# Feed-forward stages on split fp32 weights: low parts read from PSUM, high parts on GpSimd, block sums on VectorE, a fourth old-form pair

## What is computed

```python
def swiglu(x, w_in, w_out):
    a, b = jnp.split(x @ w_in, 2, axis=-1)
    return (jax.nn.silu(a) * b) @ w_out
...
x = x + 0.5 * swiglu(rmsnorm(x, norm_ffn1[i]), ffn1_w_in[i], ffn1_w_out[i])
```

## Time and profile before

| | |
|---|---|
| median of 3 runs | 3021.34 us (3018.04 to 3023.96) |
| the profiled execution | 3024.76 us, span 3023.1 us |
| TensorE busy | 2721.4 us, 90% of the span |
| VectorE busy | 2184.2 us, 72% |
| ScalarE busy | 1185.7 us, 39% |
| Pool busy | 1352.3 us, 45% |
| mean granted TensorE clock | 0.959 |

### The profile page before, as it was taken

One profiled execution on the slowest core, in us unless ns is written; L12 is line 12 of the kernel. 1 busy time (PEld: TensorE's weight loads), 2 busy tenths in 40 slices (PEclk: granted clock), 3 DMA queues, 4 the chain that ended last, 5 costly groups with the idle time before them and its releaser, 6 DMA issues. The chain is left out here.

```text
span 3023.1 us, 49541 instructions
## 1 busy us (share of the span) xinstructions
PE 2721.4 (90%) x18986; PEld 2568.8 (85%) x18986; DVE 2184.2 (72%) x2760; ACT 1185.7 (39%) x2075; POOL 1352.3 (45%) x1029
## 2 busy tenths in 40 slices
PE   7899999899888999998899999889897978899997
PEld 7899898788788989997899998677786868899996
DVE  8999966765659899848998974352625248999965
ACT  5454444222134445444454442122122224454452
POOL 4666634542328666415666632130303016666621
PEclk9999999999989999999999999989998989999998
DMA  3223222121112322321222222412323222222221
GB/s 114 81 83 96 83 96 70 51 71 52 42 59 69 93 81 82 96 90 57 74 94 92 78 91 104 150 65 105 113 81 137 86 96 66 75 86 94 85 88 60
DMA packets 110192, 255.77 MB, mean 85 GB/s; under 512 B 12624, under 2 KB 37344, under 8 KB 109968
## 3 DMA queue, kind: packets, MB, share of 16 engines
q1 hardware_dynamic: 97344, 206.73, 21.2%
q0 software_dynamic: 12624, 45.98, 4.2%
HBM read 227.88 MB, written 24.77 MB: 84 GB/s over the span
## 5 line engine op out<-in xcount | busy, mean ns | idle before, releaser
L1752 DVE TENSOR_TENSOR wl<-raw,wh 128x512 fp32r<-128x512 f32 (+1 forms) x372 | 389.4, 1047 | 82.0 <-ACT wh L1219 81.3
L938 PE MATMUL ps<-ff_x_high,wh 128*128 128x288 f32 x1216 | 365.9, 301 | 1.2 <-DVE ff_c L1780 0.2
L1523 DVE TENSOR_TENSOR wl<-raw,wh 128x1024 fp32r<-128x1024 f32 x161 | 213.4, 1325 | 210.0 <-ACT wh L1060 208.9
L938 PE MATMUL ps<-ff_x_low,wh 128*128 128x288 f32 x1216 | 364.9, 300 | 0.0
L938 PE MATMUL ps<-ff_x_high,wl 128*128 128x288 f32 x1216 | 363.6, 299 | 0.0
L2376 POOL TENSOR_TENSOR ff_w_sums<-raw,ff_w_sums 128x512 f32<-128x512 f32 (+1 forms) x124 | 158.1, 1275 | 418.3 <-DVE wl L1752 384.1
L556 PE MATMUL ps<-xh,wh 128*128 128x288 f32 x1248 | 301.4, 324 | 33.6 <-DVE xl L1545 19.9
L938 PE MATMUL ps<-ff_x_high,ff_more_high 128*128 128x288 f32 x912 | 278.4, 305 | 55.7 <-DVE ff_hidden L1789 41.7
L1060 ACT ACTIVATE wh<-raw 128x1024 fp32r<-128x1024 f32 x161 | 169.6, 1054 | 320.9 <-PE ps L534 191.2
L556 PEld LDWEIGHTS ps<-xh,wh 128*128 128x128 f32 x1248 | 207.7, 197 | 82.7 <-issue 60.5
L938 PE MATMUL ps<-ff_x_low,ff_more_high 128*128 128x288 f32 x912 | 275.3, 302 | 0.0
(11 more groups left out here) (331 smaller groups left out, 7405.3 us busy)
## 6 DMA issues: line engine op xcount, KB each, us to landing
raw<-in_w SPq DMA_DIRECT2D x161, 512.0 KB, 3.5
raw<-in_w SPq DMA_DIRECT2D x304, 256.0 KB, 2.7
raw<-in_w SPq DMA_DIRECT2D x192, 192.0 KB, 2.4
rS<-in_s_ret POOLq DMA_DIRECT2D x32, 512.0 KB, 6.5
out_ret_s<-rS POOLq DMA_DIRECT2D x32, 512.0 KB, 3.4
x<-in_xT SPq DMA_DIRECT2D x8, 288.0 KB, 6.4
out_yT<-x SPq DMA_DIRECT2D x8, 288.0 KB, 2.2
S<-in_s_hgrn POOLq DMA_DIRECT2D x4, 512.0 KB, 3.5
```

The costliest lines, as they stand in the source:

```text
L938: last = nc.tensor.matmul(bank(w, q), lhsT=slot(w, q, wt)[:, t], rhs=rhs, start=(k == 0 and (wt, r) == (0, 0) and q in (1, 5, 2)), stop=(k ...
L1523: nc.vector.tensor_tensor(wl[:, n.mod(2), :], raw[:, n.mod(NRAW), :], wh[:, n.mod(2), :], ALU.subtract)\
L1752: nc.vector.tensor_tensor(slot(w, q, 1)[:, c], src[:, c], slot(w, q, 0)[:, c], ALU.subtract)\
```

## The change

It has four parts, all in the feed-forward stages.

- ScalarE makes only high parts 1 and 2. It copies all seven weight blocks of a unit, still fp32, into a ring of the three free PSUM banks (`lift`), one bank each; a copy waits until the low part three places earlier has been made.
- VectorE's `low` reads the block from that ring in place of `raw` or `ff_w_sums` (except products 1, 5 and 6 of a stage's first unit).
- Pool makes high parts 3, 7, 5, 4 and 6 (`high`, a copy that rounds). VectorE makes the hidden-block sums that Pool made (`hidden_sums`).
- `HEAD` is 8: a fourth pair in old form, and one "in" unit fewer (30 units). Cycle 2 now also treats the first tile of the third pair. In cycles 1 and 2 VectorE does all four low parts of blocks ahead of `low(ahead, 1)`.

```diff
-HEAD, PART, TAIL = 6, 6, 4
+HEAD, PART, TAIL = 8, 6, 4
...
+LIFT_ORDER = in_order(((1, 3), (0, 2), (-1, 1), (0, 7), (-1, 5), (0, 4), (-1, 6)))
...
+    def lift_slot(w, q):
+        return ps[:, LIFT_ORDER[w.v % N_UNITS, q] % 3, :]
...
-    def pair_at(units, c):
+    def pairs_at(units, c):
...
+        steps = [(0, True, True)] if c == 1 else [(2, True, True)] if c == 2 else []
...
+            def lift(w, q):
...
+                at = LIFT_ORDER[w.v % N_UNITS, q]
+                k, q_before = LIFTED[at - 3]
+                lo_ready(act, units[k], q_before)
...
+                nc.scalar.activation(lift_slot(w, q)[:, c], src[:, c], ACT.Copy)\
+                    .then_inc(S("hi_made" if q in (3, 4) else "lifted"), 1)
...
-                src = {1: half(w.n, 0), 2: half(w.n, 1), 4: half(w.n + 1, 1), 7: half(w.n + 1, 0),
-                       5: wsum[:, 0, :], 6: wsum[:, 1, :], 3: wsum[:, 2, :]}[q]
+                if w is units[0] and q in (1, 5, 6):
+                    src = {1: half(w.n, 0), 5: wsum[:, 0, :], 6: wsum[:, 1, :]}[q]
+                else:
+                    src = lift_slot(w, q)
...
+                if not closes(older):
+                    for j, first, second in steps:
+                        if first:
+                            hidden_sums(j, 0)
+                        if second:
+                            hidden_sums(j, 1)
+                        if first and second and c <= 2:
+                            blocks_low(j, 0, 0)
+                            blocks_low(j, 0, 1)
+                            blocks_low(j, 1, 0)
+                            blocks_low(j, 1, 1)
                 if ahead:
                     low(ahead, 1)
...
+                if w.v:
+                    product_done(pool, before(w), q)
...
+                nc.gpsimd.tensor_copy(slot(w, q, 0)[:, c], src[:, c]).then_inc(S("pool_high"), 1)
...
-                if first:
-                    hidden_sums(j, 0)
-                if second and not closes(older):
-                    hidden_sums(j, 1)
```

More of the change, by code:

```diff
@@ L1197, in high @@
             def high(w, q):
                 c = slice(0, w.pairs * P)
[L1200 to L1214, removed]
+                src = source(w, q)
@@ L1307, in ffn @@
                 if new:
[L1308 to L1314 removed]
+                    lift(new, 7)
+                if not closes(older):
+                    for j, first, second in steps:
+                        if first:
+                            blocks_high(j, 0, 0)
+                            blocks_high(j, 0, 1)
+                        if second:
+                            blocks_high(j, 1, 0)
+                        if first and second:
+                            blocks_high(j, 1, 1)
                     for t in tail_at(units, c):
@@ L1319, in ffn @@
                 if ahead:
-                    high(ahead, 5)
+                    lift(ahead, 5)
                 if closes(old):
                     silu(old, 0)
-                if second and not closes(older):
-                    blocks_high(j, 1, 1)
+                if not closes(older):
+                    for j, first, second in steps:
+                        if second and not first:
+                            blocks_high(j, 1, 1)
                 if new:
-                    high(new, 4)
+                    lift(new, 4)
                 if ahead:
-                    high(ahead, 6)
+                    lift(ahead, 6)
             plain_high(NTILE - 1)
@@ L1869, in ffn @@
                 new, old, older, ahead = stage(units, c)
-                j, first, second = pair_at(units, c)
+                steps = pairs_at(units, c)
                 if old:
                     first_sum(old)
-                if second and closes(older):
-                    blocks_low(j, 1, 0)
-                    blocks_low(j, 1, 1)
-                if old:
                     low(old, 3)
-                if older and older.kind == "in" and not closes(older):
+                if closes(older):
+                    for j, first, second in steps:
+                        blocks_low(j, 1, 0)
+                        blocks_low(j, 1, 1)
+                elif older and older.kind == "in":
                     gated_a(older)
@@ L1911, in ffn @@
                     gated_a(old)
+                    if old.j < 3 * PART:
+                        hidden_sums(old.j - 1, 1)
                 else:
@@ L1916, in ffn @@
                         low(new, 4)
-                    if second and not closes(older):
-                        blocks_low(j, 1, 1)
+                    if not closes(older):
+                        for j, first, second in steps:
+                            if second and not (first and c <= 2):
+                                blocks_low(j, 1, 1)
                     if old:
```

201 lines of the change are left out of this document (130 added, 71 removed).

## The result

The changed kernel takes 2997.36 us (median; 2996.45 to 2999.48) beside 3022.24 us for the kernel before in the same comparison: ratio 0.992, 95% interval 0.9908 to 0.9933, 24.9 us less. The forecast was 2990 with 2915 to 3040.

The account below looks back on a forecast made before the run. VectorE, late because its two-SBUF-input low parts take turns with Pool, was taken to hold up TensorE; 10.2 - 12.2 - 2.4 - 3.4 = -7.8 us a stage, -31 over four, from 3021.3 gave 2990 us, range 2915 to 3040.

Parts of the forecast that it names:

- price of a low part from PSUM: VectorE's 512-column low part with its block in PSUM: 0.68 us, 0.60 from start to start, upper bound 0.74.
- Pool's copy: Pool's rounding copy of 512 columns: 0.64 us, with bounds of 0.53 and 1.30; 0.47 for 384 columns.
- rival 2: Pool becomes the bound if a rounding copy costs what a sum costs (1.30 us): 3140 us, chance 0.17.
- The head: Start of each stage: two more old pieces cost TensorE +12.7 us, the wait of 3.47 shrinks to about 1.0: +10.2.
- The first part: Product 1 to product 6 of the first "out" unit: three "in" units for four, 46.5 us for 58.7, -12.2 a stage.
- rival 1: VectorE finds the port free more often, half of its turns with Pool fall away: 2939 us, chance 0.25.
- The crowded cycles: Second and third parts, cycles with four sums and three block low parts: 1.6 us wait, -1.2 each, -2.4 a stage.
- The beginnings of "out" units: Second and third parts, 10.0 us with three products before; `add_half` now ends at 8.3: -1.7 each, -3.4 a stage.
- each longer wait costs twice: TensorE runs slow behind a longer wait: behind one of 3.42 us 16 matmuls in 3.4 us, ahead of it 28.

Follow-up runs that it names:

- `add_half` run: Changed kernel, behind a closing unit `add_half` ahead of low part 3 on VectorE and ScalarE's lift of block 3 ahead of two block high parts: 2976.57 us.

## Why the prediction was right, and where its terms were off

**Parts and prices.** The price of a low part from PSUM (0.68) and that of Pool's copy (0.64, measured 0.61) were right, and Pool did not become the bound. The run with SBUF sources shows that the source is what steadies the low part, as the prediction had it. The run with doubled copies shows about where rival 2 would have gone: 3178 us at 1.2 us a high part, dearer than the 3140 that I had for 1.30 (it makes two operations of one, and each can be held up).

**The head.** +10.2 was right: the wait left is 0.97, as expected, and from the stage's first old-form matmul to product 1 it is 48.8 us where it was 38.2, +10.6.

**The first part.** The forecast of 46.5 us was 2.6 too long; it measures 43.9, -14.8 in place of -12.2. The step that was mis-sized is the wait at the end of cycle 1, 5.2 expected and 2.70 measured; at the end of cycle 2 it was 5.8 and 5.40. I let every block sum and block low part pass one of Pool's pending operations. The rows of cycle 1 show that Pool had none for part of the time: it waits 1.42 us for TensorE, and among the block sums and block low parts it is the first sum and the last two low parts that are stretched. Together they take 7.0 us (948.71 to 955.67) where I had 9.5. That much of rival 1 came true, at this place only.

**The crowded cycles.** -1.2 each was about right: 1.46 and 0.38 us of wait for 1.62 and 1.21, -1.0 a part.

**The beginnings of "out" units.** Product 6 begins 8.4 us behind the closing unit's last product (1080.48 less 0.30, to 1088.61), 8.3 forecast. But the term of -1.7 each was wrong all the same. Before, the half speed lay behind product 1, inside these 10.0 us, in front of another wait. Now the long wait stands at product 6, and the half speed behind it is lost in full: 15 matmuls of 0.24 us in place of 0.13, 1.6 us. Counted to product 2 of the "out" unit the beginning takes 14.4 us (1080.18 to 1094.61) where it took 14.9 (1095.14 to 1110.01), -0.4 in place of -1.7. The prediction said that each longer wait costs twice and did not apply it to the wait that it moved. The `add_half` run shows the price by itself: behind waits of the same length, its beginnings with half speed take 1.1 to 1.5 us longer than those without. It also shows that not every wait costs twice.

**The sum.** From the first old-form matmul to the last one of the units the four stages are 8.5, 7.6, 5.3 and 8.5 us shorter, 7.5 on average where 7.8 was forecast. That it came so close is luck in part. In the second stage the head is +10.6, the first part -14.8, the crowded cycles -2.0, the beginnings -0.9, and -0.5 lies elsewhere: the 2.6 us that the first part gained beyond the forecast and the 2.5 that the beginnings fell short of it cancel. Between the second and the third stage 2.1 us are lost in code that the change does not touch; why stays open. The 7 us between 2990 and 2997 are 2.7 by which the forecast gain of 31 exceeds the 28.3 between the profiled executions, 3.4 that I took off because the profile of before lay above its median, and 0.9 by which that of after lies below its own.

**What the forecast did not see** is how much hangs on the fourth pair. It was costed as 12.7 us of TensorE work against one unit less, nearly neutral, and my theory for the runs with HEAD 6 followed from that; in the lists tried, both runs refute it. Why it counts for so much stays open in part: Pool's lead is read from the trace, and Pool's older order at the head was not run with three pairs. The sum came out because it was made for the lists as they stand, with HEAD 8.

## What to carry to other kernels

A two-input VectorE operation that runs beside a busy GpSimd can be made steady by putting one input into PSUM, if ScalarE has time for the copy and a bank is free. Undo each part of such a change by itself: here the gain was gone without the PSUM source, without the sums on VectorE and without the fourth pair, and the fourth pair alone cost time. And when a wait moves, follow the next wait to its place and look for half speed behind it there; the changes of order that this led to, without any change of work, gave more (42 us) than the change itself.

## What the runs showed of the hardware

A low part of 512 columns takes no longer from PSUM than from SBUF: 0.68 in the median and at most 0.70 us (the changed kernel, both widths counted), against 0.69 for low part 3 in the run with SBUF sources, while Pool was idle. The page "VectorE: DVE Perf Modes" of the Trainium skill, section "The TRN2 errata", lets expect 65 ns more; the rows do not show it, and that the sum with it, 2997, is the measured time is chance. What the trace does show, spread where both inputs are in SBUF and none where one is in PSUM, agrees with the page "SBUF — State Buffer", section "Who interferes with whom", by which only the former contends with GpSimd.

Pool's rounding copy costs 0.61 us for 512 columns where its two-input sum costs 1.30, less than half. For 384 columns it costs 0.50, so 0.86 ns a column and 0.17 us besides. The "GPSIMD Engine Reference" of the Trainium skill, section 4.1, calls one-input forms roughly line-rate; at one column a cycle of that page's 1.2 GHz this gives an estimate of 0.83 ns a column and 0.43 us for 512. The slope agrees with it, the time of the whole copy does not, and the measurement decides.

In the changed kernel TensorE's clock was at 0.50 to 0.64 behind every one of its waits from 3.88 to 5.40 us (0.54 and 0.50 behind these two), and at 1.00 behind those of 1.5. In between the length of the wait does not tell: behind 2.7 us the clock was at 1.00 at 957.89 and at 0.57 at the same place of the fourth stage, and behind 2.0 us in the `add_half` run it was at 1.00 four times and at 0.54 to 0.72 four times.
